# Two-block diffusion-style transformer step on one core: modulation chunks moved, the mixers' opening reordered, the mLSTM's maxima spread by transfers

## The reference

```
m_t = maximum(inter, Dm_i)             # running maximum per head and token
P   = qk_i * exp(D_i - m_t)
h   = num / maximum(|den|, exp(-m_t))
```

## Time and profile before

| what | value |
|---|---|
| median of 3 runs | 1808.94 us (1808.0 to 1812.43) |
| the profiled execution | 1810.99 us, span 1809.2 us |
| TensorE busy with matmuls | 1714.5 us, 95% of the span |
| VectorE busy | 1286.6 us, 71% |
| ScalarE busy | 743.7 us, 41% |
| mean granted TensorE clock | 0.986 |
| DMA | 329.77 MB, mean 182 GB/s |

### The profile page before, as it was taken

How to read it: one execution, slowest core, us unless ns; L and a number is a source line. 1 busy time by engine, 2 the same in 40 slices (tenths; PEclk the granted TensorE clock), 3 DMA queues, 4 the chain that set the end, 5 groups by cost and what they waited for, 6 DMA issues and landing times. The chain is left out here.

```text
span 1809.2 us, 30057 instructions
## 1 busy us (share of the span) xinstructions
PE 1714.5 (95%) x12816; PEld 1496.0 (83%) x12816; DVE 1286.6 (71%) x1938; ACT 743.7 (41%) x971; POOL 6.3 (0%) x14
## 2 busy tenths in 40 slices
PE   2999989999999999998899999999989999999998
PEld 2999979877999989998888789998834556747898
DVE  7876787856877786677976568897794778326744
ACT  2433375333533453335642264343322445224354
POOL 0000000000000000000000000000000000000000
PEclk9999999999999999999999999999989999999999
DMA  9877535443577737662546147774373010321102
GB/s 390 347 279 280 195 117 222 166 161 117 233 279 293 289 141 279 248 264 94 205 155 240 68 169 278 281 277 183 149 280 129 1 47 1 126 95 47 47 24 93
DMA packets 48516, 329.77 MB, mean 182 GB/s; under 512 B 5224, under 2 KB 8448, under 8 KB 9344
## 3 DMA queue, kind: packets, MB, share of 16 engines
q1 hardware_dynamic: 47520, 324.69, 46.7%
q0 software_dynamic: 864, 3.17, 0.6%
HBM read 326.77 MB, written 1.07 MB: 181 GB/s over the span
## 5 line engine op out<-in xcount | busy, mean ns | idle before, releaser
L332 PE MATMUL ps<-xhi,low 128*128 128x256 f32 x2048 | 501.1, 284 | 4.2 <-ACT xhi L1390 4.2
L332 PEld LDWEIGHTS ps<-xhi,low 128*128 128x128 f32 x2048 | 362.4, 192 | 5.9 <-ACT xhi L1390 5.2
L332 PE MATMUL ps<-xhi,whi_wk 128*128 128x256 f32 x1072 | 297.8, 287 | 39.8 <-ACT xhi L1390 38.9
L1390 ACT ACTIVATE wk<-ps 128x256 f32<-128x256 f32 (+5 forms) x219 | 108.6, 504 | 490.5 <-PE ps L332 425.0
L332 PE MATMUL ps<-xa,ring 128*128 128x256 f32 (+1 forms) x1056 | 287.0, 430 | 10.0 <-issue 4.8
L332 PE MATMUL ps<-xlo,whi_wk 128*128 128x256 f32 x1072 | 290.6, 280 | 0.0
L332 PEld LDWEIGHTS ps<-xa,ring 128*128 128x128 f32 x1056 | 200.4, 192 | 91.1 <-issue 62.0
L1390 ACT ACTIVATE whi_wk<-ring 128x2048 fp32r<-128x2048 f32 x100 | 191.5, 1918 | 159.2 <-DMA ring<-in_stream_dram 95.3
L332 PEld LDWEIGHTS ps<-xhi,whi_wk 128*128 128x128 f32 x1072 | 202.6, 194 | 42.8 <-issue 41.1
L1967 DVE TENSOR_TENSOR low<-ring,whi_wk 128x2048 fp32r<-128x2048 f32 (+1 forms) x101 | 228.4, 2264 | 6.6 <-ACT whi_wk L1390 6.6
L332 PE MATMUL ps<-wk 64*64 64x64 f32 (+10 forms) x2712 | 210.3, 262 | 5.8 <-ACT wk L1390 4.3
(11 more groups left out here) (131 smaller groups left out, 2547.9 us busy)
## 6 DMA issues: line engine op xcount, KB each, us to landing
ring<-in_stream_dram SPq DMA_DIRECT2D x302, 1024.0 KB, 5.6
ring<-in_cond_dram SPq DMA_DIRECT2D x2, 1024.0 KB, 4.8
wk<-spread_dram POOLq DMA_DIRECT2D x4, 384.0 KB, 5.2
wk<-spread_dram POOLq DMA_DIRECT2D x2, 768.0 KB, 7.5
tab<-in_tab_dram SPq DMA_DIRECT2D x1, 1440.0 KB, 20.4
res<-in_xt_dram SPq DMA_DIRECT2D x1, 1024.0 KB, 17.5
res<-in_ct_dram SPq DMA_DIRECT2D x1, 1024.0 KB, 9.2
out_dram<-wk SPq DMA_DIRECT2D x4, 256.0 KB, 2.4
```

What stands on the lines that cost most here:

```text
L332: last[0] = nc.tensor.matmul(o, l, r, start=start, stop=stop, skip_group_check=free)
L1390: return nc.scalar.activation(o, i, f, **kw)
```

## The change

1. **Modulation chunks.** Of the 16 late chunks, (7, 0..5) are worked in the FFN m = 3, one in each of rounds 2 to 7 (`FFN_MODS`); (6, 8..11), (7, 6) and (7, 7) stay in MLA's opening, two in each of three places; (7, 8..11) come at MLA's end (`LAST_MODS`): one behind each of the second to fourth output chunk and the last behind the loop. `cond2` is loaded and activated four times, not twice.
2. **Mixers' opening.** `l2` stands behind the sixth projection and `p6.0`; `rows` behind one more `win_low`; the wait for the last three projections' readers stands ahead of `qk`, not ahead of `pairs`.
3. **Pieces placed anew.** For m = 0 and 3, the first split of the mixer's weights moves from the norm's start into the FFN's round of w13 chunk 20, and `normed` from the norm's end to behind `win_high(m, 4)`; VectorE no longer waits for it there.
4. **Maxima and stabilisers.** The nine pieces `lm` and `lb` issue no matmul. GpSimd stores the rows of the maxima and stabilisers (two small stores), and after TensorE's `x 6` reads `l_em` (two transfers of 384 KB), after `y 6` `l_w` (768 KB). ScalarE and VectorE work on them in place. `lm0` and `lm1` change places with `p11.1` so that one projection half less stands ahead of `y 6`.

```diff
-             "mt3", "p5.0", "mo1", "p5.1", "p11.0", "p11.1"]
-          + ["lm0", "lm1", "lm2", "lb0", "lb1", "ls0", "ls1", "lb2", "lx0", "lb3", "ls2", "lb4", "lb5", "ls3", "ls4", "q15", "lx1", "ls5", "lx2"])
+             "mt3", "p5.0", "mo1", "p5.1", "p11.0", "lm0", "p11.1", "lm1"]
+          + ["lm2", "lb0", "lb1", "ls0", "ls1", "lb2", "lx0", "lb3", "ls2", "lb4", "lb5", "ls3", "ls4", "q15", "lx1", "ls5", "lx2"])
...
-        LATE_MODS = [(6, ch) for ch in range(GATE, 12)] + [(7, ch) for ch in range(12)]
-        LATE_AT = (0, 2, 4, 7, 10, 13, 16)
+        FFN_MODS = [(7, ch) for ch in range(6)]
+        LATE_MODS = [(6, ch) for ch in range(GATE, 12)] + [(7, 6), (7, 7)]
+        LATE_AT = (0, 1, 2, 3, 4, 5, 6)
+        LAST_MODS = [(7, ch) for ch in range(GATE, 12)]
...
+                    if m == 3 and 2 <= p < 8:
+                        leave("ada", *FFN_MODS[p - 2])
...
+                    if kind in ("lm", "lb"):
+                        return
...
-                    elif kind == "lm":
-                        p = int(what)
-                        for h in (2 * p, 2 * p + 1):
-                            mm(half(beside(s, 256), h), each(ident[:, ROW_I + h:ROW_I + h + 1], 64)[:, 0, :], r_nm, True, True, free=True)
-                    elif kind == "lb":
-                        h = int(what)
-                        mm(beside(s, 256), each(ident[:, ROW_I + h:ROW_I + h + 1], 128)[:, 0, :], r_max, True, True)
                     elif kind == "ls":
                         h = int(what)
                         o = beside(s)
+                        eng.wait_ge(*step_of("fread", m, BESIDE.index("p11.1")))
...
-                    if i == 4:
-                        for p in range(3):
-                            eng.wait_ge(*step_of("proj_read", m, p))
-                        eng.wait_ge(scalar_done, step("l2sq", m))
-                        for t in range(6):
-                            mm(banks(1, 1536)[:, 256 * t:256 * t + 256], blk, tiles(g_sq, 256)[:, t], True, True)
-                        last[0].then_inc(tensor_done, 1)
-                        done.named("l2", m)
-                fill(2)
+                fill(1)
+                for p in range(3):
+                    eng.wait_ge(*step_of("proj_read", m, p))
+                eng.wait_ge(scalar_done, step("l2sq", m))
+                for t in range(6):
+                    mm(banks(1, 1536)[:, 256 * t:256 * t + 256], blk, tiles(g_sq, 256)[:, t], True, True)
+                last[0].then_inc(tensor_done, 1)
+                done.named("l2", m)
+                fill(1)
...
+                    if kind == "w13" and j == 20 and f == 0:
+                        win_high(m + 1, 0)
...
-                        eng.wait_ge(tensor_done, step("beside", m, s))
-                        act(l_em[:, 256 * p:256 * p + 256], beside(s, 256), ACT.Exp, *key).then_inc(scalar_done, 1)
+                        eng.wait_ge(minima_in, 32 * (l + 1))
+                        act(l_em[:, 256 * p:256 * p + 256], l_em[:, 256 * p:256 * p + 256], ACT.Exp, *key).then_inc(scalar_done, 1)
...
                 win_high(m, 4)
+                normed(m - 1)
...
-                eng.wait_ge(scalar_done, step("normed", m))
+                if m % 3:
+                    eng.wait_ge(scalar_done, step("normed", m))
...
-                        o = beside(s, 256)
-                        eng.wait_ge(tensor_done, step("beside", m, s))
-                        tt(l_w[:, h, 0:256], table("neg_t", 0, 256), o, SUB).then_inc(vector_done, 1)
-                        tt(l_w[:, h, 256:384], table("neg_t", 256 + P, P), o[:, P:T], SUB, *key).then_inc(vector_done, 1)
+                        eng.wait_ge(maxima_in, 16 * (l + 1))
+                        tt(l_w[:, h, 256:384], table("neg_t", 256 + P, P), l_w[:, h, P:T], SUB).then_inc(vector_done, 1)
+                        eng.wait_ge(vector_done, done.count)
+                        tt(l_w[:, h, 0:256], table("neg_t", 0, 256), l_w[:, h, 0:256], SUB, *key).then_inc(vector_done, 1)
...
                     if ch == 2:
+                        win_low(m, 6)
                         rows()
-                        win_low(m, 6)
...
-                for c in range(6):
+                for c in range(2):
                     mod_part(*LATE_MODS[c])
...
-                for c in range(6, 10):
+                for c in range(2, 4):
                     mod_part(*LATE_MODS[c])
...
-                for c in range(10, 16):
+                for c in range(4, 6):
                     mod_part(*LATE_MODS[c])
...
+                    if ch:
+                        mod_part(*LAST_MODS[ch - 1])
+                mod_part(*LAST_MODS[3])
...
+                eng.wait_ge(maxima_stored, 32 * (l + 1))
+                eng.wait_ge(tensor_done, step("x", m, 6))
+                for parity in range(2):
+                    eng.dma_start(tiles(l_em[64 * parity:64 * parity + 64, :], 256),
+                                  spread[l, 12:18].rearrange("(t two) n -> two t n", two=2)[parity].partition_broadcast(64)).then_inc(minima_in, 16)
+                eng.wait_ge(tensor_done, step("y", m, 6))
+                eng.dma_start(l_w[:, :, 0:256], spread[l, 18:24].partition_broadcast(P)).then_inc(maxima_in, 16)
```

More of the change, by code:

```diff
@@ L226, in build @@
         g_t, g_tt, g_dt, g_at, g_att = [W(SCR + 1536 * i, 1536) for i in range(5)]
-        r_u, r_ab, r_ln = [g_at[:, 256 * i:256 * i + 256] for i in range(3)]
+        r_u, r_ab, r_ln = W(23040, 256), W(23296, 256), r_rw
         g_sq = g_t
@@ L318, in scratch, with cond_of @@
         def scratch(m, ch):
-            return W(12800, D) if (m, ch) in LATE_MODS else W(6144, D)
+            return W(12800, D) if (m, ch) in LATE_MODS + LAST_MODS else W(6144, D)
+        def cond_of(m, ch):
+            return 0 if (m, ch) in FFN_MODS else 2 if (m, ch) in LATE_MODS else 3 if (m, ch) in LAST_MODS else 1
         block = ctx.enter_context(nc.Block())
@@ L447, in ffn @@
                         found["down", m, j] = found["down", m, j - 1] = found["chunk", held[0]]
-                    if m == 5 and p == 1:
-                        leave("cond2", 0)
+                    if m in (3, 5) and p == 1:
+                        leave("cond2", m // 5)
                     for ch in ada_of(m, p):
                         leave("ada", m + 1, ch)
+                    if m == 3 and 2 <= p < 8:
+                        leave("ada", *FFN_MODS[p - 2])
                     if m == 5 and p == 10:
@@ L662, in mixer @@
                 eng.wait_ge(scalar_done, step("ekd", m))
+                for p in range(3, 6):
+                    eng.wait_ge(*step_of("proj_read", m, p))
                 for h in [0, 2, 4, 1, 3, 5]:
@@ L846, in ada @@
                     if i == 0:
-                        leave("cond2", 1)
+                        leave("cond2", 2)
                     for c in range(LATE_AT[i], LATE_AT[i + 1]):
@@ L1098, in mla @@
                         next_sums(2 * ch - 2)
+                leave("cond2", 3)
+                for c in range(4):
+                    leave("ada", *LAST_MODS[c])
                 next_sums(6)
@@ L1506, in norm, with normed @@
                         win_high(m + 1, c)
+                if to_ffn:
+                    normed(m)
+            def normed(m):
                 g0_, b0_ = COLS["ln_g"][0] + 8 * m, COLS["ln_b"][0] + 8 * m
@@ L1525, in ffn @@
                         whole(m, c + HALVES)
[L1526 to L1527 removed]
+                    if kind == "w13" and j == 20 and f == 0:
+                        win_high(m + 1, 0)
+                    if m in (3, 5) and kind == "w13" and j == 2:
+                        conditions(m // 5)
                     if m == 5 and kind == "w13" and j == 15:
@@ L1993, in mod_half @@
                 else:
-                    eng.wait_ge(scalar_done, step("cond2", 1 if (m, ch) in LATE_MODS else 0))
+                    eng.wait_ge(scalar_done, step("cond2", cond_of(m, ch)))
                     bias = col("ada_b2", 24 * (m - 6) + col_at)
@@ L2089, in norm @@
                 elif m < 5:
-                    win_low(m + 1, 0)
                     win_low(m + 1, 1)
@@ L2171, in ffn @@
                         lows(m, c + 3)
+                    if kind == "w13" and j == 20 and f == 0:
+                        win_low(m + 1, 0)
                     if kind == "w13" and j == 20 and m in SPLIT_MODS:
@@ L2181, in ffn @@
                             mod_part(m + 1, ch)
+                        if m == 3 and 2 <= j // 2 < 8:
+                            mod_part(*FFN_MODS[j // 2 - 2])
                         if j == 19:
@@ L2702, in _ @@
                     eng.dma_start(spread[l, at_row:at_row + 6], table_rows[row:row + 6, :]).then_inc(rows_stored, 16)
+                for at_row, table_rows in ((12, r_nm), (18, r_max)):
+                    eng.dma_start(spread[l, at_row:at_row + 6], table_rows[ROW_I:ROW_I + 6, :]).then_inc(maxima_stored, 16)
                 eng.wait_ge(rows_stored, 32 * (l + 1))
```

21 lines of the change are left out of this document (10 added, 11 removed).

## The result

The changed kernel takes 1828.51 us (median of 4 runs, 1826.64 to 1830.84), the kernel before 1810.68 beside it: ratio 1.0097, 95% interval 1.0082 to 1.0112. It is slower by 17.8 us where 18.2 less was forecast. The profiled execution has a span of 1826.2, 17.0 over the 1809.2 of before.

The account below looks back on a forecast made before the run. TensorE, busy 95% of the span, was taken to bound the kernel, each stall also paid in slow clock. Terms -1.6 - 3.6 - 6.6 - 12.7 + 6.3 + 0 = -18.2 gave 1790.7 us (-1.0%), range 1783 to 1800.

Parts of the forecast that it names:

- A: Norm ahead of mixers m = 1, 4: first weight split hides in an FFN round, -0.8 each, -1.6 in all.
- B: Mixers' opening: projections fill the wait for l2, kk starts 1.8 us sooner per mixer, -3.6 in all.
- C: Maxima and stabilisers: 12 matmuls fewer (-4.9), a copy and a wait added, -3.3 per mixer, -6.6 in all.
- R1: Maxima come late: l_w needs 8.0 or more, VectorE stalls, gain there about 0 per mixer; 1797 us, chance 0.14.
- D: MLA's opening: both TensorE stalls and the slow clock behind them go, -12.7 us.
- E: MLA's end: modulation products delay xn7, TensorE's idle time grows from 3.14 to 9.4, +6.3 us.
- F: FFN m = 3: added chunks bring VectorE to 16.4 of 16.90 per round, still below TensorE, cost 0.
- R3: FFN m = 3 becomes bound by VectorE or the ring: +18 gives 1808.5, later landings about 1815; chance 0.07.
- R4: Openings hide more: no slow stretch behind chunk 7, kk -3.5 each, l_w in time; 1785 us, chance 0.08.

Follow-up runs that it names:

- the first: Changed kernel with the mixers' opening put back in its old order, the moves of normed and first split kept: 1827.07 us, ratio 1.0079.
- the third run: Changed kernel with ScalarE's copy of p6.0 moved directly behind its copy of projection 5: 1830.12 us, ratio 1.0101.
- the quiet opening: Changed kernel plus one SyncE wait: the mixer's chunk 8 is not issued before g_dt has landed: 1814.98 us, ratio 1.0014.
- a quiet ring: Changed kernel with SyncE holding chunk 8 until g_dt lands and, at the ends, the first output weights until l_w lands: both holds 1801.64 us, ratio 0.9940.
- the copy first: ScalarE's copy of p6.0 behind projection 5; with both SyncE holds and the last two modulation chunks behind xn7 in the changed kernel: 1790.39 us, ratio 0.9881.
- the old order of the opening: Changed kernel with both SyncE holds, last two modulation chunks behind xn7, and l2 back behind projection 4, rows ahead of chunk 6's low: 1786.78 us, ratio 0.9867.
- all edits: Changed kernel with both SyncE holds, ScalarE's copy of p6.0 first and the last two modulation chunks behind xn7: 1790.39 us, ratio 0.9881.
- part 1 alone: Kernel before with only the modulation-chunk part, the last two chunks behind xn7, and the changed kernel's scratch places: 1799.85 us, ratio 0.9929.
- the matmul kernels: Kernels keeping lm and lb as matmuls: part 1 alone, 1799.85 us, and all edits without maxima transfers or hold at the end, 1796.48 us.
- the holds: SyncE's waits in the changed kernel: chunk 8 until g_dt lands (alone 1814.98 us), and first output weights until l_w lands (both 1801.64 us).

## Why the prediction was wrong

**A** was right in kind: the wait in m = 1's norm fell from 1.11 to 0.47; -0.8 was the forecast, 0.6 is what the wait lost.

**B failed, first of all in what GpSimd's transfers cost.** The sentence was: "Queued behind it are GpSimd's g_dt (768 KB, 8.0 to landing), issued about 2 us later than now, and first used far behind `kk`: hidden; if not, up to 2", and nothing at all on the pairs, which VectorE reads before `kk`. Three parts of it are wrong.

- The landing. I took the 5.8 and 8.0 from the rows of before as if they belonged to the transfer. They belonged to the state of the ring: with TensorE stalled at `l2` the slots were full and SyncE had nothing to issue. The same edit that fills TensorE's stall has two chunks issued 11 us sooner, and the next two beside the reads. Measured: 10.4 and 12.7.
- The first use. `g_dt` is not first used far behind `kk`: TensorE waits ahead of `kk` for VectorE's addition to it, the very 1.76 at 288.63 that the prediction counts among the products for `kk`. In the first and the third run VectorE waits 2.46 and 2.20 for `g_dt` there.
- The issue. `rows` ended 1.5 sooner, not later (stores at 271.5 against 272.9); the reads were issued 0.5 later, because the stores took 3.2 in place of 1.7.

`kk` came 1.5 later and not 1.8 sooner, its own records took 9.36 in place of 5.92, and the clock was 0.54 and 0.60 in the windows behind the two waits: +6.2 and, against m = 1's end, +6.9 per opening, with A's gain in them, in place of -1.8. That the ring is the cause is shown by the quiet opening: 5.1 and 6.9 to landing, and 13.5 us back.

What remains of B with a quiet ring is a term that was sized wrongly. The products are then 0.5 sooner than before, and 1.5 with the copy first; with the old order of the opening they are 4.4 sooner at m = 1. So the gain is not the new order's. With the old order the wait ahead of `l2` is 2.13, not 5.23: most of that stall goes with part 3, in which VectorE no longer waits 3.65 for `normed` (no run moves `normed` alone). The prediction asked only that the input be there by 271.1, and filled a wait that had already shrunk. The new order leaves `l2` until 270.4 and puts the wait ahead of `p7.0`: 4.0 was the forecast, for the low of chunk 7, and 6.31 were measured, ended by ScalarE's copy of `p6.0`, which `p7.0` needs because it is two pieces on in the same PSUM slot, and which stands behind the silus and the high of chunk 8.

**C failed by the same cost**, there written out: "I take 5.8, because the tail of the mixer loads less than the opening". The trace of before already says otherwise. In the view of DMA issues of 372 to 400, in 40 slices, the ring moves mostly 350 to 480 GB/s until about 387, so at the forecast issue of 377.7 the DMA engines were busy. The first line is of the kernel before, the second of the changed one:

```profile
GB/s 316 433 398 421 480 398 386 421 374 351 386 129 222 410 421 398 70 164 386 386 421 94 0 0 0 0 0 0 23 0 0 0 0 0 0 0 0 0 0 0
...
GB/s 410 82 12 0 0 0 0 35 176 281 410 421 445 398 421 322 269 240 263 287 293 339 398 345 357 351 404 415 398 439 427 421 398 211 35 0 0 0 0 0
```

In the changed kernel ring and transfers are in flight together from about 380 to 395, the ring's own chunks need 9.9 and `l_w` 10.6, later than the 8.0 that I had as the upper bound. VectorE waits 5.37, TensorE 5.55 and then works 6.9 us at clock 0.50, half of 6.72 lost: +6.6 at m = 1. At m = 4 `l_w` took 7.9, within that bound, VectorE waited 2.69 and TensorE 2.87; the clock was 0.50 from 1020 to 1028, and the end cost 3.8 where the bound had +0.5. So the price of the slow stretch behind a wait was too low as well. Rival R1 named this mechanism, at 1797, with the same two prices. `l_em`, put down as read "far ahead of use", made ScalarE wait 5.00; no run shows whether that cost anything.

The removed matmuls were also worth less than the 4.3 of an undisturbed end: ends of 100.0 with a quiet ring against 101.0, so 1.0, and 98.4 and 100.0 with all edits, so 2.6 and 1.0. The windows show a clock of 0.93 in such an end; in the end with matmuls it was 1.00 (the window of 383 to 408 above, behind the ring's last loads). The row is of the run with all edits:

```profile
378.00:404.00 26.00, 24.92 (x178) 19.91 (x179) 13.98 (x29) 11.73 (x22) 0.00 (x0) 0.93 0.49 193
```

That the twelve matmuls had covered TensorE's small waits for VectorE's copies, and that their absence brings the clock down, fits these rows and one idle time of 0.65; it is argued and not tested, and the matmul kernels' own ends of 104.2 and 104.3 show that such an end can lose clock too.

**D** was right in its mechanism and size: both stalls gone, 12.9 forecast as 12.7 (with E's +6.3 it makes the -6.6 of the table), and part 1 alone is 12.4 faster. **E** was right: idle time 9.46, forecast 9.4; undoing it gave 6.8. **F** was right: 16.35 of 16.90 on VectorE, forecast 16.4, the rounds keep their 16.9, and the DMA share is 0.79 where 0.86 was worked out. R3, the rival that led to a slower kernel, was the wrong one: I looked for the loss where engines were nearly full and not where a transfer had its time from an idle queue. Three small sums of the prediction don't come out, and nothing hangs on them: R4 with D's lower bound is 1784.5, not 1783; R3's 18 us give 1808.7; and the chances of "faster" add up to 0.89, not 0.87.

The two rules of the Trainium skill that stood beside C can now be read against the runs. DMA: Bandwidth & Descriptors (section Anatomy of one DMA — SWDGE (gpsimd) path) gives 3.8 us for 768 KB as an estimate; measured were 4.6 to 4.9 at the ends with a quiet ring, 6.8 to 7.7 in the openings with a quiet ring, where the pairs are in flight too, and 7.9 to 15.4 with a busy ring. So it is below all of them, nearest to the first, and no forecast beside a loaded ring. SBUF — State Buffer (the "DVE blocks DMA" trap) would have certain VectorE operations hold up GpSimd's descriptors. The quiet ring changed nothing in VectorE's program and the landing of `l_w` fell to 4.6, and in the changed kernel VectorE stood idle for the last 5.37 us of the landings at 288 and 394; so no more than a small rest can be due to that here.

Open stays why the changed kernel with the old opening varied from 1819.7 to 1829.4, and how much of each late landing is queueing behind chunks already issued and how much is sharing with those issued later; the holds remove both. That the sharing alone can do it is seen in the run with the old opening: nothing was in flight ahead of its reads, and they took 8.0 and 14.4 beside chunks issued with them.

## What to carry to other kernels

The time from issue to landing in a profile is a property of the moment, not of the transfer: before using such a row, look at what fills the queues then, and ask whether the edit moves another queue's loads onto it. Filling a compute engine's stall also frees buffers sooner and starts their loads sooner; if a small transfer on which the next step waits lived in the gap, it loses its gap. And when one change has two edits against the same stall, work out what each leaves for the other: here the stall fell to 2.13 without the new order, and the new order, which filled it, moved a wait to `p7.0` and left the products 3.0 later. A wait on the bulk queue, which costs nothing while the ring is ahead, can give it back: here one line was worth 13 us at the openings, and a second one 13 at the ends.

## What was not expected of the hardware

- A store of 6 KB issued beside the ring's 1 MB loads took 3.1 to 4.3 us to land, 1.6 to 2.1 with none beside it; reads of 384 KB 7.0 to 10.4 against 5.1 to 5.9, and of 768 KB 7.9 to 15.4 against 4.6 to 8.1. The upper figures of the quiet side are openings in which the ring starts again before the landing, or other reads are in flight.
- 256 KB beside the ring took 6.7, more than the 4.6 to 4.9 of 768 KB at the same place without it.
- `kk`'s 48 records took 5.92 at full clock and 9.36 to 10.48 where 1.64 to 4.01 us of idle time stood ahead of them and another 9 to 13 us earlier; with only the earlier one (the quiet opening, 6.41) they took 5.92.
